# Seven half-size products (Strassen) in place of eight for 42 of the 44 gate/up blocks of a SwiGLU layer

## The chip, the core and the metric

The kernel runs on one core of a Trainium2 chip. The metric is the device time of one execution in microseconds (us), as a median over runs; lower is better. The engines that matter are TensorE (PE, with its weight loads as PEld), VectorE (DVE), ScalarE (ACT), GpSimd (POOL) and the DMA queue that SyncE (SP) feeds. TensorE writes to PSUM, eight banks of 128x512 fp32; all other data lies in SBUF.

## What is computed

One transformer layer on 512 tokens of width 2048 (batch 1, depth 1), fp32 throughout: forgetting attention with four heads, a residual add, then the part that is changed:

```python
D_FF = 5632                                   # -(-8 * 2048 // 768) * 256
h = _rmsnorm(x, norm_ffn)                     # 512 x 2048
gu = h @ w_gate_up                            # 2048 x 11264
g, u = gu[..., :D_FF], gu[..., D_FF:]
x = x + (jax.nn.silu(g) * u) @ w_down         # 5632 x 2048
out = _rmsnorm(x, final_norm)
```

## The kernel before

Every fp32 operand of a matmul is kept as two fp32r parts, high and low: ACT copies it to the high part (a rounding), DVE subtracts the high part from the operand and writes the low part. A product is then three matmuls for each tile of 128 of the contraction: high by high, high by low, low by high (`PASSES`, in `products`, L841). One matmul instruction has a stationary operand of 128x128 and a moving one of up to 512 columns, and each has its own weight load.

The feed-forward part works in 11 groups of 4 blocks. A block is 128 columns of the gate and the same 128 of the up projection. Its result is transposed: 128 features on the partitions, 512 tokens in the columns of a PSUM bank, so that the weights are stationary and the tokens (`hT`, 16 tiles of 128 x 512) move: 2 x 16 x 3 = 96 matmuls of 512 columns. Then ACT takes silu of the gate from its bank into `tmp` (L591), DVE multiplies by the up bank (L817), ACT makes the high part of the activation (L594) and DVE the low part (L820). After four blocks comes the down projection: for each quarter `cb` of the output's 2048 columns and each quarter `tb` of the tokens 4 x 3 matmuls of 512 columns, 192 for a group, and DVE adds each bank to the residual stream `xres` (L772).

Weights come as slabs of 128x2048 fp32 (1 MB): SP loads one into the next of 3 `raw` buffers (L305), ACT (`split_hi`, L422) and DVE (`split_lo`, L617) make the two parts in the next of 2 `split` buffers, and TensorE uses it. A gate slab has all of the contraction, the up slab is the next one, and a down slab is 4 tiles of 128x512. The order on each engine is the order of the code; each engine waits on semaphores that count. The groups run in hardware loops (`Fori`), the first and last apart. In the first group the two slabs of block 0 are multiplied in token halves, matmuls of 256 columns (`EARLY`, `LATE`), because the second half of `hT` (transposed by TensorE at L854, high part L427, low part L624) comes late. After the last group's down projection POOL, ACT and DVE do the final norm: squares (L552), weights (L402), `rstd` (L410), scaling (L803, L807, L584), and 16 stores.

Of the kernel before, what the change touches and what calls it, by code (L numbers as in the profile page):

```python
# [27 lines left out]
P = 128  # L28
SLAB = 2048
# [29 lines left out]

def fox_layer(nc, x, norm_mix, w_in, b_f, w_out, norm_ffn, w_gu, w_down, norm_out, out):  # L60
# [34 lines left out]
    with ExitStack() as ctx:  # L95
# [9 lines left out]

        hT = [sb(f"hT_{n}", [P, ND, S], F32R) for n in ("hi", "lo")]
# [4 lines left out]
        tmp = sb("tmp", [P, 4, BANK])  # L111
        ident = sb("ident", [P, P])
        bound = sb("bound", [P, P])

        with nc.sbuf_tensor("xres", [P, NT, D], F32) as xres, nc.sbuf_tensor("gain", [P, D], F32) as gain:
            pass
# [3 lines left out]
        vT = sb("vT", [P, NH, S])  # L120
        decay_t = sb("decay_t", [P, S], F32R)
        decay_s = sb("decay_s", [P, S], F32R)
        decay_h = sb("decay_h", [P, S], F32R)

        rows = sb("rows", [P, H, 4])
        row_of = sb("row_of", [P, 8])
        head_of = sb("head_of", [P, H])
        wf = sb("wf", [P, ND, H])
        bf_all = sb("bf_all", [P, H])
        bf = sb("bf", [P, 1])  # L130
        half = sb("half", [P, 1])
# [4 lines left out]
        negmax = sb("negmax", [P, NT])  # L136
        rowsum = sb("rowsum", [P, NT])
        rinv = sb("rinv", [P, NT])
# [10 lines left out]

        x_in = [sem(f"x_in{i}") for i in range(NT)]  # L150
# [3 lines left out]
        raw_in = [sem(f"raw_in{i}") for i in range(RAW)]  # L154
        out_done = sem("out_done")
# [46 lines left out]

        y_done = sem("y_done")
# [71 lines left out]

        def wait_used(eng, at):


            n = at.off
            if n < FIRST_WO:  # L280
                eng.wait_ge(slab_used, at.per * at.i + (n + 1))
            elif n < FIRST_FFN:
                cb, second = divmod(n - FIRST_WO, 2)
                if second:
                    eng.wait_ge(y_done, NT * (cb + 1))
                else:
                    eng.wait_ge(slab_used, FIRST_WO + cb + 1)
            else:
                j = n - FIRST_FFN
                if j < 2 * G:  # L290
                    eng.wait_ge(slab_used, (2 * G) * at.i + (FIRST_WO + NC + j + 1))
                else:
                    eng.wait_ge(y_done, (NT * NC) * at.i + (NT * NC + NT * (j - 2 * G + 1)))

        def slab(parts, at, part, tile, cols):

            return parts[part][:, at.ring, tile * cols:(tile + 1) * cols]
# [3 lines left out]
        def _(sp):  # L301
# [32 lines left out]
            with sp.Fori(0, GROUPS) as g:  # L334
                at = At(FIRST_FFN, FFN, g)
                for j in range(2 * G):
                    a = at.plus(j)
                    load(a, tile_of(a, P), w_gu_v[:, :, bass.ds(g * (G * P) + ((j // 2) * P + (j % 2) * F), P)])
                for cb in range(NC):
                    a = at.plus(2 * G + cb)  # L340
                    load(a, tile_of(a, BANK), w_down_v[:, bass.ds(g * G, G), cb * BANK:(cb + 1) * BANK])
# [8 lines left out]
        def _(pool):  # L350
# [47 lines left out]
            for cb, tb in LAST_DOWN:  # L398
                v1 = var[:, tb:tb + 1]
                pool.wait_ge(sq_done, squared(cb, tb))  # L400
                if cb < NC - 1:
                    nc.gpsimd.tensor_tensor(out=y(tb, cb), in0=y(tb, cb), in1=gain[:, cb * BANK:(cb + 1) * BANK],  # L402
# [14 lines left out]
        def _(act):  # L417
# [6 lines left out]
            def take_hT(norm, tb, chunks=range(NC)):  # L424
                for q in chunks:
                    act.wait_ge(h_turned, 4 * NT * norm + 4 * tb + q + 1)
                    nc.scalar.activation(hT[0][:, 4 * q:4 * q + 4, tb * P:(tb + 1) * P],  # L427
# [147 lines left out]
            wait_normalised(act, 1, NT - 1, OWN[1] - 1)  # L575
            wait_normalised(act, 1, NT - 1, NC - 1)
            act.dma_start(gain[:], norm_out.partition_broadcast(P)).then_inc(gain_in, 16)
# [9 lines left out]
            def ffn(g, last=False):  # L587
                at = At(FIRST_FFN, FFN, g)
                for f in range(G):
                    wait_used(act, at.plus(2 * f))  # L590
                    nc.scalar.activation(tmp[:, f % 2, :], ps[:, GU[f % 2][0], :], ACT.Silu).then_inc(silu_done, 1)  # L591
                    split_hi(at.plus(2 * f + 2))
                    act.wait_ge(a_done, G * g + (f + 1))
                    nc.scalar.activation(oT[0][:, f, :], tmp[:, 2 + f % 2, :], ACT.Copy).then_inc(a_hi, 1)  # L594
                    split_hi(at.plus(2 * f + 3))
                if not last:
                    for cb in range(NC):
                        split_hi(at.plus(2 * G + 2 + cb))
                    return
                for cb, tb in LAST_DOWN:  # L600
                    if cb < NC - 2 and tb == 0:
                        split_hi(at.plus(2 * G + 2 + cb))
                    if cb:
                        act.wait_ge(sq_done, squared(cb - 1, tb))
                    square(NT * NC * GROUPS + nth(cb, tb), cb, tb, tmp[:, tb, :])
                    finish_before(cb, tb, finish)

            with act.Fori(0, GROUPS - 1) as g:
                ffn(g)
            ffn(GROUPS - 1, last=True)  # L610
# [3 lines left out]
        def _(dve):  # L614
# [5 lines left out]
            def take_hT(norm, tb):  # L620
                for q in range(4):
                    n = 4 * NT * norm + 4 * tb + q
                    dve.wait_ge(hT_hi, n + 1)
                    nc.vector.tensor_tensor(hT[1][:, 4 * q:4 * q + 4, tb * P:(tb + 1) * P],  # L624
                                            ps[:, turned(norm, tb, q)[0], :].rearrange("p (c t) -> p c t", t=P),
                                            f32(hT[0][:, 4 * q:4 * q + 4, tb * P:(tb + 1) * P]),
# [465 lines left out]
```

## Time and profile before

| what | value |
|---|---|
| median of 3 runs | 1889.2 us (1889.04 to 1890.01) |
| span of the profiled execution, first to last instruction | 1885.3 us |
| matmuls, all with a weight load | 8536 |
| PE busy, PEld busy, DVE busy, ACT busy, POOL busy | 1866.9, 1552.6, 664.1, 474.5, 58.6 us |
| feed-forward part | from about 436 us to the end |
| DMA | 188 MB, 100 GB/s over the span |

The busy time of PE is the union of durations that overlap (one matmul lasts longer than the step to the next), so steps are read from start to start. "Idle before" is the time in which an engine had nothing to run just before an instruction, with the one that released it.

### The profile page before, as it was taken

The page shows a single profiled execution, that of the slowest core. Times are in us where ns is not written, and L with a number is a line of the kernel's source. Part 1 is how long each engine was busy: PE and PEld are TensorE (multiplying, and loading weights), DVE is VectorE, ACT ScalarE, POOL GpSimd, SP SyncE. Part 2 cuts the span into 40 slices and gives each one's busy share as a digit, 9 for nine tenths or more (in the row PEclk, how much of TensorE's full clock was granted, in tenths as well). Part 3 has the DMA queues.
Part 4 walks back from the last instruction along what each step waited for, and adds up shares of the span by engine and source line. Part 5 has one row for each costly group of instructions (what it writes and reads, how often), then busy time and mean ns, then how long its engine had stood idle before and what let it go on. Part 6 is the DMA issues. An engine that isn't in the chain of part 4 may idle for free.

```text
span 1885.3 us, 20299 instructions
## 1 busy us (share of the span) xinstructions
PE 1866.9 (99%) x8536; PEld 1552.6 (82%) x8536; DVE 664.1 (35%) x637; ACT 474.5 (25%) x482; POOL 58.6 (3%) x82
## 2 busy tenths in 40 slices
PE   8999999999999999999999999999999999999998
PEld 6888888888888888888888888888888888888886
DVE  5333332435242242342332332422333333234234
ACT  5223222334212222222222222222221221221224
POOL 3000000012000000000000000000000000000005
PEclk9999999999999999999999999999999999999999
DMA  7333232433333233333233333332333323323322
GB/s 224 90 89 83 73 89 89 179 90 103 99 90 109 92 90 103 97 89 110 90 89 103 97 89 109 92 89 101 99 89 110 90 89 110 90 89 110 91 89 90
DMA packets 266289, 188.22 MB, mean 100 GB/s; under 512 B 5264, under 2 KB 234640, under 8 KB 265360
## 3 DMA queue, kind: packets, MB, share of 16 engines
q1 hardware_dynamic: 263856, 181.45, 32.4%
q10 hardware_dynamic: 2400, 6.29, 0.9%
q8 instruction: 25, 0.41, 0.1%
q14 instruction: 8, 0.07, 0.0%
HBM read 183.54 MB, written 4.19 MB: 100 GB/s over the span
## 4 chain that ended last, share of the span: by engine, by line
PE 96%; DVE 2%; ACT 1%; POOL 1%; issue 1%; DMA 0%; ACTq 0%; POOLq 0%
PE ps L841 95%; DVE tmp L636 1%; POOL xres L402 0%; DVE hT_lo L624 0%; PE ps L854 0%; DMA xres<-in_x_dram 0%; DVE split_lo L617 0%; PE ps L896 0%; DVE xres L772 0%; ACT oT_lo L500 0%; ACT split_hi L422 0%; PE ps L886 0%; ACT hT_hi L427 0%; PE ps L877 0%; ACT tmp L552 0%
## 5 line engine op out<-in xcount | busy, mean ns | idle before, releaser
L841 PE MATMUL ps<-hT_hi,split_hi 128*128 128x512 f32 (+1 forms) x1840 | 706.8, 384 | 0.8 <-DVE split_lo L617 0.8
L841 PE MATMUL ps<-hT_lo,split_hi 128*128 128x512 f32 (+1 forms) x1840 | 706.0, 384 | 0.0
L841 PE MATMUL ps<-hT_hi,split_lo 128*128 128x512 f32 (+1 forms) x1840 | 706.0, 384 | 0.0
L617 DVE TENSOR_TENSOR split_lo<-raw,split_hi 128x2048 fp32r<-128x2048 f32 x164 | 375.9, 2292 | 579.9 <-ACT split_hi L422 579.9
L422 ACT ACTIVATE split_hi<-raw 128x2048 fp32r<-128x2048 f32 x164 | 313.1, 1909 | 378.7 <-PE ps L841 374.8
L841 PEld LDWEIGHTS ps<-hT_hi,split_hi 128*128 128x128 f32 x1840 | 345.9, 188 | 68.4 <-issue 1.0
L841 PEld LDWEIGHTS ps<-hT_hi,split_lo 128*128 128x128 f32 x1840 | 345.9, 188 | 68.0
L841 PEld LDWEIGHTS ps<-hT_lo,split_hi 128*128 128x128 f32 x1840 | 345.9, 188 | 67.6
L841 PE MATMUL ps<-split_hi,oT_hi 128*128 128x512 f32 x832 | 324.3, 390 | 0.6 <-issue 0.4
L841 PE MATMUL ps<-split_hi,oT_lo 128*128 128x512 f32 x832 | 323.9, 389 | 0.0
L841 PE MATMUL ps<-split_lo,oT_hi 128*128 128x512 f32 x832 | 323.9, 389 | 0.0
L772 DVE TENSOR_TENSOR xres<-ps,xres 128x512 f32<-128x512 f32 x192 | 131.0, 688 | 201.1 <-PE ps L841 201.1
L841 PEld LDWEIGHTS ps<-split_hi,oT_hi 128*128 128x128 f32 x832 | 156.2, 188 | 33.6 <-issue 0.8
L841 PEld LDWEIGHTS ps<-split_hi,oT_lo 128*128 128x128 f32 x832 | 156.2, 188 | 32.4
L841 PEld LDWEIGHTS ps<-split_lo,oT_hi 128*128 128x128 f32 x832 | 156.2, 188 | 32.3
L594 ACT ACTIVATE oT_hi<-tmp 128x512 fp32r<-128x512 f32 x44 | 27.8, 632 | 400.1 <-DVE tmp L817 400.1
L817 DVE TENSOR_TENSOR tmp<-ps,tmp 128x512 f32<-128x512 f32 x44 | 30.4, 691 | 265.9 <-PE ps L841 265.9
L591 ACT ACTIVATE tmp<-ps 128x512 f32<-128x512 f32 x44 | 26.3, 598 | 339.1 <-PE ps L841 339.1
L402 POOL TENSOR_TENSOR xres<-xres,gain 128x512 f32<-128x512 f32 x12 | 18.2, 1539 | 1409.2 <-ACT tmp L552 1409.1
L820 DVE TENSOR_TENSOR oT_lo<-tmp,oT_hi 128x512 fp32r<-128x512 f32 x44 | 30.5, 693 | 30.7 <-ACT oT_hi L594 30.7
L678 DVE SCALAR_TENSOR_TENSOR kT_lo<-ps,kT_hi 128x512 fp32r<-128x512 f32 x8 | 5.5, 691 | 60.9 <-ACT kT_hi L466 60.9
L636 DVE SCALAR_TENSOR_TENSOR tmp<-xres,rstd,gain 128x512 f32<-128x512 f32 x20 | 20.9, 1094 | 12.3 <-POOL rstd L387 12.3
(105 smaller groups left out, 454.5 us busy)
## 6 DMA issues: line engine op xcount, KB each, us to landing
raw<-in_ffn_w_gate_up_dram SPq DMA_DIRECT2D x88, 1024.0 KB, 5.7
raw<-in_ffn_w_down_dram SPq DMA_DIRECT2D x44, 1024.0 KB, 5.0
raw<-in_fox_w_in_dram SPq DMA_DIRECT2D x24, 1024.0 KB, 5.8
raw<-in_fox_w_out_dram SPq DMA_DIRECT2D x8, 1024.0 KB, 5.1
xres<-in_x_dram SPq DMA_DIRECT2D x4, 1024.0 KB, 8.2
xres<-in_x_dram ACTq DMA_DIRECT2D x4, 1024.0 KB, 8.5
out_dram<-xres SPq DMA_DIRECT2D x16, 256.0 KB, 3.1
gain<-in_norm_mix_dram SPq DMA_DIRECT2D x1, 1024.0 KB, 6.9
```

Of the source, the lines that this page charges most:

```text
L402: nc.gpsimd.tensor_tensor(out=y(tb, cb), in0=y(tb, cb), in1=gain[:, cb * BANK:(cb + 1) * BANK], op=ALU.mult).then_inc(weighted, 1)
L422: nc.scalar.activation(split[0][:, at.ring, :], raw[:, at.raw, :], ACT.Copy).then_inc(hi_ready, 1)
L591: nc.scalar.activation(tmp[:, f % 2, :], ps[:, GU[f % 2][0], :], ACT.Silu).then_inc(silu_done, 1)
L594: nc.scalar.activation(oT[0][:, f, :], tmp[:, 2 + f % 2, :], ACT.Copy).then_inc(a_hi, 1)
L617: nc.vector.tensor_tensor(split[1][:, at.ring, :], raw[:, at.raw, :], f32(split[0][:, at.ring, :]), ALU.subtract).then_inc(lo_ready, 1)
L636: nc.vector.scalar_tensor_tensor(tmp[:, q, :], y(tb, q), rstd[:, tb:tb + 1], gain[:, q * BANK:(q + 1) * BANK], ALU.mult, ALU.mult).then_in ...
L678: nc.vector.scalar_tensor_tensor(lo, ps[:, PROJ[j % 2], :], SCALE if j < NH else 1.0, f32(hi), ALU.mult, ALU.subtract).then_inc(qk_done, 1)
L772: nc.vector.tensor_tensor(part, ps[:, bank, :], part, ALU.add).then_inc(added, 1)
L817: nc.vector.tensor_tensor(a, ps[:, GU[f % 2][1], :], tmp[:, f % 2, :], ALU.mult).then_inc(a_done, 1)
L820: nc.vector.tensor_tensor(oT[1][:, f, :], a, f32(oT[0][:, f, :]), ALU.subtract).then_inc(a_ready, 1)
L841: ins = nc.tensor.matmul(bank, stationary(sp, t), moving(mp, t), start=first and t == tiles[0] and (sp, mp) == PASSES[0], stop=last and t ...
```

## The change

Block 0 stays as it was (now `early`), and block 1 is multiplied as before, but from slabs of half the size (`plain_part`). The 42 others go through `unit`. Tokens are cut in two halves of 256 and the contraction in two halves of 1024 (A11, A12 for the first tokens, A21, A22 for the others; first digit tokens, second contraction). The weights of a block are cut in the two halves of the contraction and in gate and up (B11, B12 gate and up of the first half, B21, B22 of the second). The seven products (`SEVEN`) are, in order and with the bank that each goes to (numbers relative to a start that rotates by block):

A11·B11 (0), S1·(B11+B12) (1), S2·(B11+B12+B22) (0), S4·B22 (2), S3·(B12+B22) (0), A12·B21 (3), A22·(B11+B12+B22+B21) (0)

with S1 = A21-A22, S2 = S1-A11, S3 = A11-A21, S4 = A12+S2. Bank 0 goes on accumulating over four of them. Each is 8 tiles by 3 passes, 24 matmuls of 256 columns, 168 for a block; the order of the passes is now 16 with the high weights, then 8 with the low ones. The four sums of tokens, with high and low parts, are made once, by DVE and ACT, while blocks 0 and 1 and the first unit run. They lie where the attention's buffers lay (`S1`, `S2` in `oT`, `S3` in `s3`, `S4` in the second ring buffer of `split`); `hT` gets another layout in the second norm (`h_ffn`), and the activations lie over A21.

The sums of weights are four in-place adds of 128x1024 for a block on DVE (`sum_of`, L1231). The high and low parts are made for each of the seven weight operands (`part_hi` L853, `part_lo` L1217, 128x1024) in a ring of two half-size buffers. DVE and ACT combine the products in pieces of 128x256: `copy_q` (L872), four adds or subtractions on DVE (L1282, L1287, L1292, L1297), silu in two halves (L878, L883). SP loads half-size slabs (512 KB) into 6 slots, each load behind a wait on `t_lo` or `t_sum`. The down projection of all groups but the last uses half-size slabs too (two tiles of the contraction for all four `tb`, then the other two); the last one uses full slabs as before. The final gain is now loaded by ACT after the last activation, not at the start of the feed-forward part.

```diff
+        SEVEN = ((A11, 0), (S1, 1), (S2, 0), (S4, 2), (S3, 0), (A12, 3), (A22, 0))
...
+            def half_product(at, e):
+                tokens, which = SEVEN[e]
+                n = at.first + e
+                out = ps[:, bank_of(at.u, which), 0:HALF]
+                fresh = which or e == 0
+                pe.wait_ge(t_hi, at.part(e))
+                for k in range(QK8):
+                    for part in range(2):
+                        ins = nc.tensor.matmul(out, ring(0, n)[:, k * P:(k + 1) * P],
+                                               tokens[part][:, k * HALF:(k + 1) * HALF],
...
+                ins.then_inc(highs_read, 1)
+                pe.wait_ge(t_lo, at.part(e))
+                for k in range(QK8):
+                    ins = nc.tensor.matmul(out, ring(1, n)[:, k * P:(k + 1) * P],
+                                           tokens[0][:, k * HALF:(k + 1) * HALF],
...
+                ins.then_inc(product, 1)
...
+            def part_hi(r, n, source):
+                if n >= 2:
+                    if n - 2 < n_unit_parts(r):
+                        act.wait_ge(highs_read, highs(r, n - 1))
...
+                nc.scalar.activation(ring(0, n), source, ACT.Copy).then_inc(t_hi, 1)
...
+            def unit(at, before, then):
+                if before:
+                    gate_two(before)
+                sum_hi(at, 2)
+                copy_q(at, 0)
+                if before:
+                    act_hi(at.r, before.u, ga[:, :])
+                plain_hi(at.r, at.first + 3, "B22", at.u)
+                copy_q(at, 1)
+                sum_hi(at, 4)
+                plain_hi(at.r, at.first + 5, "B21", at.u)
+                sum_hi(at, 6)
...
+            def part_lo(r, n, source):
+                dve.wait_ge(t_hi, parts(r, n + 1))
+                if n >= 2:
+                    if n - 2 < n_unit_parts(r):
+                        dve.wait_ge(product, products_done(r, n - 1))
...
+                nc.vector.tensor_tensor(ring(1, n), source, f32(ring(0, n)), ALU.subtract).then_inc(t_lo, 1)
...
+            def sum_of(at, into, other):
+                x1, x2 = (slot(place(at.r, name, at.u)[0]) for name in (into, other))
+                nc.vector.tensor_tensor(x1, x1, x2, ALU.add).then_inc(t_sum, 1)
...
-            ffn(0, first=True)
-            with pe.Fori(1, GROUPS - 1) as g:
-                ffn(g)
-            ffn(GROUPS - 1, last=True)
+            for n in range(4):
+                plain_part(n, GU[1][n // 2], n % 2)
+            group(None)
+            with pe.Fori(0, GROUPS - 2) as r:
+                group(r)
```

On TensorE, where one slab or product of a block ends and the next begins. Before, in the last group (`hT` tokens, `split` weights):

```order
L841 MATMUL ps<-hT_hi,split_hi 128x512
L841 MATMUL ps<-hT_lo,split_hi 128x512
L841 MATMUL ps<-hT_hi,split_lo 128x512
L841 MATMUL ps<-hT_hi,split_hi 128x512 [waits lo_ready]
L841 MATMUL ps<-hT_lo,split_hi 128x512
```

The change at the same place, between the first and the second of the seven products (S1 lies in `oT`):

```order
L1635 MATMUL ps<-hT_hi,split_hi 128x256
L1635 MATMUL ps<-hT_lo,split_hi 128x256
L1642 MATMUL ps<-hT_hi,split_lo 128x256 [waits t_lo]
L1642 MATMUL ps<-hT_hi,split_lo 128x256 x7
L1635 MATMUL ps<-oT_hi,split_hi 128x256 [waits t_hi,combined]
L1635 MATMUL ps<-oT_lo,split_hi 128x256
```

The columns of a matmul are halved, and there are two places with waits in each 24 matmuls where there was one in 48.

On DVE, what one block asks for. Before, the block that begins with the second row here, in the last group:

```order
L617 TENSOR_TENSOR split_lo<-raw,split_hi 128x2048 [waits hi_ready]
L817 TENSOR_TENSOR tmp<-ps,tmp 128x512 [waits slab_used,silu_done]
L820 TENSOR_TENSOR oT_lo<-tmp,oT_hi 128x512 [waits a_hi]
L617 TENSOR_TENSOR split_lo<-raw,split_hi 128x2048 [waits hi_ready] x2
```

The change, the first ten operations of a block that follows another (`ga` and `cc` are the gate and up results, `qq` the two copied products):

```order
L1217 TENSOR_TENSOR split_lo<-raw,split_hi 128x1024 [waits product,t_hi]
L1231 TENSOR_TENSOR raw<-raw 128x1024 [waits part_in4,t_lo]
L1254 TENSOR_TENSOR ga<-ga,cc 128x512 [waits silu_done]
L1217 TENSOR_TENSOR split_lo<-raw,split_hi 128x1024 [waits product,t_hi]
L1259 TENSOR_TENSOR hT_lo<-ga,hT_hi 128x512 [waits a_hi]
L1217 TENSOR_TENSOR split_lo<-raw,split_hi 128x1024 [waits product,t_hi]
L1231 TENSOR_TENSOR raw<-raw 128x1024 [waits t_sum]
L1282 TENSOR_TENSOR cc<-qq,ps 128x256 [waits a_done,product,q_copied]
L1217 TENSOR_TENSOR split_lo<-raw,split_hi 128x1024 [waits product,t_hi]
L1287 TENSOR_TENSOR cc<-ps,cc 128x256 [waits combined,product]
```

Two low parts and two operations on the activation became seven low parts, four sums, four combinations and the two operations, each behind a wait on ACT, on TensorE or on DVE itself.

On DVE at the start of the feed-forward part. Before, the last low parts of `hT` are followed by the first low part of weights:

```order
L624 TENSOR_TENSOR hT_lo<-ps,hT_hi 128x4x128 [waits hT_hi] x8
L830 UNCONDITIONAL_BRANCH
L830 ISA
L617 TENSOR_TENSOR split_lo<-raw,split_hi 128x2048 [waits hi_ready]
```

The change, the first of four pieces of the sums of tokens, and the start of the second:

```order
L1015 TENSOR_TENSOR hT_lo<-ps,hT_hi 128x4x128 [waits hT_hi] x8
L1338 TENSOR_TENSOR sy<-hT_hi,hT_lo 128x512 [waits hT_done]
L1338 TENSOR_TENSOR qq<-hT_hi,hT_lo 128x512
L1338 TENSOR_TENSOR sy<-qq,sy 128x512 [waits s_sum]
L1338 TENSOR_TENSOR sz<-hT_hi,hT_lo 128x512
L1343 TENSOR_TENSOR oT_lo<-sy,oT_hi 128x512 [waits s_hi]
L1338 TENSOR_TENSOR sy<-sy,sz 128x512 [waits s_lo,s_sum]
L1338 TENSOR_TENSOR qq<-sz,qq 128x512
L1343 TENSOR_TENSOR oT_lo<-sy,oT_hi 128x512 [waits s_hi]
L1338 TENSOR_TENSOR sy<-hT_hi,hT_lo 128x512 [waits s_lo]
```

Three such pieces stand ahead of the first low part of weights for block 1, and the fourth and S4 between the parts of block 1 and those of the first unit.

## Rows read from the trace of the kernel before

**Rows 1.** The page: busy time by engine, and the chain that ended last

```profile
PE 1866.9 (99%) x8536; PEld 1552.6 (82%) x8536; DVE 664.1 (35%) x637; ACT 474.5 (25%) x482; POOL 58.6 (3%) x82
PE 96%; DVE 2%; ACT 1%; POOL 1%; issue 1%; DMA 0%; ACTq 0%; POOLq 0%
```

**Rows 2.** Busy time in four stretches (start:end length, busy us and count by engine)

```profile
core 0: us, PE busy (x) PEld busy (x) DVE busy (x) ACT busy (x) POOL busy (x), PEclk, DMA share, GB/s
461.80:1832.70 1370.90, 1370.90 (x6050) 1135.53 (x6050) 454.43 (x372) 296.39 (x221) 0.00 (x0) 1.00 0.33 97
```

**Rows 3.** Timeline of PE, block 0 in token halves and its end (start, duration)

```profile
447.60 0.28 PE L841 MATMUL ps<-hT_lo,split_hi 128*128 128x256 f32 x1
447.72 0.28 PE L841 MATMUL ps<-hT_hi,split_lo 128*128 128x256 f32 x1
...
461.75 0.28 PE L841 MATMUL ps<-hT_hi,split_lo 128*128 128x256 f32 x1
461.87 0.40 PE L841 MATMUL ps<-hT_hi,split_hi 128*128 128x512 f32 x1
```

**Rows 4.** Timeline of PE and PEld in an attention head, from 128 to 256 columns

```profile
144.58 0.19 PEld L841 LDWEIGHTS ps<-pT_hi,v_lo 128*128 128x128 f32 x1
144.64 0.27 PE L841 MATMUL ps<-pT_hi,v_lo 128*128 128x128 f32 x1
144.69 0.19 PEld L841 LDWEIGHTS ps<-pT_hi,v_hi 128*128 128x128 f32 x1
144.75 0.33 PE L841 MATMUL ps<-pT_hi,v_hi 128*128 128x256 f32 x1
144.80 0.19 PEld L841 LDWEIGHTS ps<-pT_lo,v_hi 128*128 128x128 f32 x1
144.92 0.28 PE L841 MATMUL ps<-pT_lo,v_hi 128*128 128x256 f32 x1
```

**Rows 5.** Groups by line and shape, DVE (count, busy us, mean ns, idle before)

```profile
L617 DVE TENSOR_TENSOR split_lo<-raw,split_hi 128x2048 fp32r<-128x2048 f32 x164 | 375.9, 2292 | 579.9 <-ACT split_hi L422 579.9
L820 DVE TENSOR_TENSOR oT_lo<-tmp,oT_hi 128x512 fp32r<-128x512 f32 x44 | 30.5, 693 | 30.7 <-ACT oT_hi L594 30.7
L666 DVE TENSOR_TENSOR pT_lo<-ps,pT_hi 128x256 fp32r<-128x256 f32 x4 | 1.7, 415 | 0.0
```

**Rows 6.** The same for ACT

```profile
L422 ACT ACTIVATE split_hi<-raw 128x2048 fp32r<-128x2048 f32 x164 | 313.1, 1909 | 378.7 <-PE ps L841 374.8 <-issue 3.8
L594 ACT ACTIVATE oT_hi<-tmp 128x512 fp32r<-128x512 f32 x44 | 27.8, 632 | 400.1 <-DVE tmp L817 400.1
L456 ACT ACTIVATE pT_hi<-ps 128x256 fp32r<-128x256 f32 x4 | 1.6, 403 | 0.0
```

**Rows 7.** Timeline of ACT and DVE at the start of the feed-forward part

```profile
436.85 1.90 ACT L422 ACTIVATE split_hi<-raw 128x2048 fp32r<-128x2048 f32 x1
438.78 2.29 DVE L617 TENSOR_TENSOR split_lo<-raw,split_hi 128x2048 fp32r<-128x2048 f32 x1 [2.59 <-ACT split_hi L422]
439.88 2.03 ACT L427 ACTIVATE hT_hi<-ps 128x512 fp32r<-128x512 f32 x4
444.40 4.86 DVE L624 TENSOR_TENSOR hT_lo<-ps,hT_hi 128x512 fp32r<-128x512 f32 x8
456.31 0.60 ACT L591 ACTIVATE tmp<-ps 128x512 f32<-128x512 f32 x1 [6.73 <-PE ps L841]
```

**Rows 8.** DMA issues (count, KB each, median us to landing)

```profile
raw<-in_ffn_w_gate_up_dram SPq DMA_DIRECT2D x88, 1024.0 KB, 5.7
raw<-in_ffn_w_down_dram SPq DMA_DIRECT2D x44, 1024.0 KB, 5.0
out_dram<-xres SPq DMA_DIRECT2D x16, 256.0 KB, 3.1
gain<-in_norm_ffn_dram ACTq DMA_DIRECT2D x1, 1024.0 KB, 14.6
```

**Rows 9.** Timeline of PE at the very start, eight equal matmuls twice

```profile
1.30 6.33 PE L934 MATMUL ps<-decay_s 128*128 128x512 f32 x8 [1.30 <-POOL half L352]
12.61 3.60 PE L934 MATMUL ps<-decay_s 128*128 128x512 f32 x8
```

**Rows 10.** The last 8 us, as in rows 2: no matmul, granted clock 0.66

```profile
1878.00:1886.00 8.00, 0.00 (x0) 0.00 (x0) 1.15 (x2) 1.68 (x4) 0.81 (x2) 0.66 0.63 206
```

**Rows 11.** Timeline at the last down projection: DVE, then POOL's first final weight

```profile
1833.04 0.69 DVE L817 TENSOR_TENSOR tmp<-ps,tmp 128x512 f32<-128x512 f32 x1 [6.22 <-PE ps L841]
1846.58 6.48 POOL L402 TENSOR_TENSOR xres<-xres,gain 128x512 f32<-128x512 f32 x4 [1402.65 <-ACT tmp L552]
```

More of the change, by code:

```diff
@@ L333, in _ @@
                 load(a, tile_of(a, BANK), w_out_v[:, kt:kt + NK // 2, cb * BANK:(cb + 1) * BANK])
[L334 to L341, printed above, removed]
+            for j in range(2):
+                load(At(FIRST_FFN + j), tile_of(At(FIRST_FFN + j), P), w_gu_v[:, :, j * F:j * F + P])
@@ new lines, in is_last, with all_units, group @@
+            def is_last(r):
+                return isinstance(r, int) and r == GROUPS - 2
+            def all_units(r):
+                every = units(r)
+                for at, before, then in zip(every, [None] + every[:-1], every[1:] + [None]):
+                    unit(at, before, then)
+            def group(r, following):
+                all_units(r)
+                at = units(r)[-1]
+                gate_two(at)
+                act_hi(r, at.u, ga[:, :])
+                for i in range(2, 2 * NC):
+                    down_hi(r, i)
+                plain_hi(following, 0, "B11", 0)
+                sum_hi(Unit(following, 0), 1)
@@ new lines, in is_last, with all_units, group @@
+            def is_last(r):
+                return isinstance(r, int) and r == GROUPS - 2
+            def all_units(r):
+                every = units(r)
+                for at, before, then in zip(every, [None] + every[:-1], every[1:] + [None]):
+                    unit(at, before, then)
+            def group(r, following):
+                all_units(r)
+                at = units(r)[-1]
+                down_lo(r, 1)
+                act_out(r, at.u, at.silu(2))
+                act_lo(r, at.u, ga[:])
+                for cb in range(NC):
+                    if cb < NC - 1:
+                        down_lo(r, 2 * cb + 2)
+                    else:
+                        unit_lo(Unit(following, 0), 0)
+                        first_sum(Unit(following, 0))
+                    for tb in range(NT):
+                        add(y_before(r) + nth(cb, tb, last=False), cb, SC[tb], tb)
+                    if cb < NC - 1:
+                        down_lo(r, 2 * cb + 3)
@@ new lines, in _, with last_down @@
+            group(None)
+            with pe.Fori(0, GROUPS - 2) as r:
+                group(r)
+            r = GROUPS - 2
+            for at in units(r):
+                unit(at)
+            def last_down(cb, tb, tiles, start=True, stop=True):
+                return products(ps[:, down_bank(cb, tb, True), :],
+                                lambda part, k: aT[part][:, k, tb * P:(tb + 1) * P],
+                                lambda part, k: split[part][:, LAST_RING[cb], k * BANK:(k + 1) * BANK],
+                                tiles, first=start, last=stop)
```

662 lines of the change are left out of this document (556 added, 106 removed), and 3 rows, old and new, of the table LOADS.

## The prediction

> **What bounds the kernel now.** I read the page first: PE is busy 99% of the span and has 96% of the chain that ended last, DVE is busy 35% and ACT 25% [rows 1]. So the time is TensorE's, and busy time says nothing of its pace, since one matmul lasts longer than the step to the next. Hence the stretches: from the end of block 0 to the end of the last block TensorE starts 6050 matmuls in 1370.9 us with no idle time [rows 2]. That is 43 blocks of 96 and 10 down projections of 192, 6048 by the code: a step is 0.2267 us for 512 columns, a block takes 96 x 0.2267 = 21.76 us, a down projection 43.5 us. Then the one place where gate and up are already multiplied with 256 columns, from 447.60 to 461.87: 119 steps in 14.27 us, 0.1199 us each [rows 3]. This is the row on which the gain hangs. Half of 0.2267 would be 0.1133: a matmul has a part of some 0.013 us that doesn't halve.
>
> **The main term.** A changed block has 7 x 24 = 168 matmuls of 256 columns: 168 x 0.1199 = 20.15 us, against 21.76. That is 1.61 us less, not the 2.72 us that an eighth would be. For 42 blocks: 67.8 us. The down projections keep their 192 matmuls of 512 columns; block 0 and block 1 keep theirs.
>
> Can weight loads keep up? A load lasts 0.19 us, more than the new step. But in an attention head loads start every 0.11 us (144.58, 144.69, 144.80) [rows 4], so they overlap, and 0.12 is within their pace, narrowly. Were they unable to, a block would take 168 x 0.188 = 31.6 us; the rows exclude it.
>
> Each product adds two places with waits, 14 for a block, 588 in all. In rows 3 three changes of operand with waits lie inside the 119 steps and are in their mean. The nearest row that speaks for a cost is the step from 144.75 to 144.92, 0.17 us for 256 columns, 0.05 more than the next ones [rows 4]; it comes after 128-column matmuls, where the load was late. I take 0 and keep 0.05 x 588 = 29 us for the range.
>
> The Trainium skill ("TensorE: Matmul & The Clock Gate", Back-to-back issue gap) gives a step of N/2.4 ns plus 2.5 ns. By it 512 columns take 215.8 ns and 256 take 109.2 ns, and 42 blocks would save 42 x (20.72 - 18.35) = 99.6 us. The trace doesn't agree: 226.7 and 119.9 ns.
>
> **Can DVE and ACT feed it?** Durations: DVE 2.292 us for 2048 columns, 0.693 for 512, 0.415 for 256 [rows 5]; the line through the first two gives 1.23 for 1024. ACT 1.909, 0.632 and 0.403 [rows 6], so 1.06 for 1024. Bounds for 1024 on DVE: half of 2.292 (1.15) and two of 512 (1.39). Per block DVE does 7 low parts, 4 sums, 4 combinations, and the product and low part of the activation: 11 x 1.23 + 4 x 0.42 + 2 x 0.69 = 16.6 us of 20.15 (82%). ACT: 7 x 1.06 + 4 x 0.40 + 0.63 = 9.7 us. Both fit, so what decides is the order. I lay out one block, TensorE's product e beginning at 2.88e. Its high weights are free at +1.92, its bank is readable at +3.05 (a matmul's end is 0.16 after the next step); the high part of e+2 waits for the first, the low part of e+2 for the second.
> - From the block before: product 5 readable at -2.7, combination to -2.3, low part of product 0 to -1.05, first sum to 0.2.
> - ACT high part 1 to 1.3, DVE low 1 to 2.5, second sum to 3.7.
> - ACT high part 2 to 4.8 (needed at 5.76), the copy of product 0 to 5.2 (needed at 5.76: slack 0.6), DVE multiplies the old activation meanwhile, low 2 to 6.0 (needed 7.7).
> - ACT high 3 to 6.8, DVE low 3 to 8.0 (needed 10.6), third sum to 9.2, ACT high 4 to 10.3 (needed 11.5), low 4 to 11.5.
> - Product 3 is readable at 11.7, and from here DVE waits for TensorE again: low 5 to 13.3 (needed 16.3), fourth sum 14.6, ACT high 6 to 15.6 (needed 17.3).
>
> TensorE waits for nothing; the smallest slack is 0.6 us and is built on eleven hand-overs. A hand-over is short: ACT ends at 438.75 and DVE begins at 438.78, and DVE kept its 2.29 us while ACT worked beside it [rows 7]. DMA: the loads for the next block are issued at 9.2 to 14.6 and needed 13 us later; a half slab must land between the 3.1 us of 256 KB and the 5.7 us of 1 MB [rows 8]. In the down projection a half slab is worth 5.4 us of TensorE, against one high part, one low part and two adds for it; hidden. I take 0 for the steady state.
>
> **The start.** DVE is free at 449.3 (444.40 + 4.86) [rows 7]; TensorE needs the first parts of block 1 at 461.87 [rows 3]. Ahead of them stand three of four pieces of token sums. A piece is 9 operations of 0.69 and, since nearly each waits for ACT or for the one before, about 6.4 us: 449.3 + 5.6 + 6.4 + 6.4 = 467.7; then ACT's copies of the last S3 piece and of the first weights: 469.3. TensorE waits 7.4 us. After it blocks run to 491.1. DVE goes on: two low parts (471.9), the fourth piece and S3 (479.4), activation of block 0, and two low parts with four pieces of S4 of about 3.5 us (three operations, a copy, a low part), first weights of the unit, a sum, activation of block 1: 500.3. ACT has the second high part at 499.9, so the unit's second product begins there and not at 494.0, and the third at 504.1 after sum, high part and copy. Without waits the third would begin at 461.87 + 21.76 + 5.76 = 489.4. Loss: 14.7 us. DVE's whole list here is some 45 us of work; at the 0.60 of eight low parts in 4.86 us [rows 7] it is 5 us shorter, and with 0.1 more for each of 52 hand-overs 5 us longer: 9 to 20 us.
>
> The clock: after some 4 us without a matmul it had fallen at the end (0.66 over 8 us in which the last matmul had ended about 1876.5, the rest at full speed) [rows 10], which is from 2.4 to 1.2 GHz. At the start eight equal matmuls took 6.33 us, later 3.60 [rows 9]: a restart costs 2.7 us. After the first wait that falls into the second one and costs nothing; after the second, 3.5 us long by then, 0 to 2.7. I take 0.
>
> **The end.** DVE has in its list the low part of the second full down slab (2.29 us) ahead of the low part of the last activation: 1.6 us after the last product ACT has silu, then 1.9 of high part, 0.6 of activation, and DVE is done about 5.7 us after the last product, where TensorE has two banks of nine matmuls, 4.1 us, to go on with. Loss 1.5 us; before there was none. The final gain is issued about 3.5 us after the last product and needed by POOL 13.8 us after (1846.58 against 1832.8) [rows 11]: 6.9 us would do, 14.6 [rows 8] would be 4 late, on a POOL list that lies near the end. I take 0, keep 4.
>
> **Sum.** -67.8 + 14.7 + 1.5 = -51.6 us. On the profiled span, 1885.3 to 1833.7; the median lies 3.9 us over the span, so 1837.6, say 1838 us.
>
> **Rivals.**
> - *The waits between products show.* Each costs about 0.05 us, or the 0.6 us of slack in a block is used up by hand-overs and TensorE waits 0.5 to 0.7 us in each block: +21 to +29, 1859 to 1867 us. For it: two operations at each point where there was one in 48 matmuls, register arithmetic in the loop, three engines in turn. Against: 0.1199 includes waits.
> - *The step halves.* With the tokens now contiguous and the weights high ones first, 0.1133 us: 168 x 42 x 0.0066 = 46 us less, 1792. Rows 3 speak against it, since the same instruction takes 0.1199 there. The 109.2 ns of the Trainium skill's page would go this way too.
> - *DVE becomes the bound, and it is slower than before.* Mechanism: from product 5 of a block to high part 4 of the next DVE has seven operations of 1024 in a row, with three high parts on ACT between them, and 1.2 us of slack (10.3 against 11.5). Above 1.40 us for an operation on DVE TensorE waits in each block; at 1.58 us it waits 1.23 us, and 42 of these take all of the 51.6. At 1.65 us: 7 x 0.42 - 1.2 = 1.74, x 42 = 73, so 1911 us. It would take an add in place, or DVE under ACT, PE and DMA at once, to be a third slower than the line of rows 5. Against: rows 7, and the upper bound of 1.39 us, at which nothing waits yet.
>
> **How the numbers follow.** Forecast 57%, its own range 1828 to 1852 (start 9 to 20, clock 2.7, gain 4, step 0.1195 to 0.1203). Waits that show 22%. Step halves 6%. DVE bound and slower than before 9%. The other 6% is a mix between forecast and before. 0.2% (3.8 us) is about what can be told from no change. Faster 0.89, same 0.02, slower 0.09. The range leaves out the halved step, the slower case and the far end of the waits: 1823 to 1872.
>
> **What would show it.** 11,560 matmuls (8536 + 42 x 72), a step of 0.120 in the units, 20.15 us from block to block in a group and 124.1 us for a group (130.6 now); DVE busy about 1150 us, from 664. PE idle in two gaps near 462 and 494, 7.4 and 3.5 to 6 us, with the clock down after the first. A wait of TensorE on DVE or ACT that recurs in each block would be the third rival; steps of 0.12 with a longer one at each first matmul the first. If TensorE's idle time is small and the span is still above 1850, the step is wrong.

## The result, and the profile after

The median goes from 1889.1 us to 1840.3 us (four runs of each, 1838.7 to 1841.4 after); the ratio is 0.974, 95% interval 0.973 to 0.976. The forecast was 1838, its range 1823 to 1872. The profiled execution has a span of 1839.3 us.

First the page of the changed kernel, as in [rows 1]: busy time by engine, and by engine the chain (the work that ended last, followed back from the end of the span):

```profile
PE 1807.1 (98%) x11560; PEld 1647.4 (90%) x11560; DVE 1115.5 (61%) x1277; ACT 659.0 (36%) x867; POOL 58.5 (3%) x82
PE 92%; DVE 4%; ACT 2%; issue 1%; POOL 1%; DMA 0%; ACTq 0%; POOLq 0%; DVEq 0%
```

The 11,560 matmuls are there, and the chain has still 92% on TensorE. Where it waits is in the view of waits (engine, line, waited for: us in total, times, longest):

```profile
PE ps L1617 <- ACT split_hi L853: 7.5, 1, 7.5
PE ps L1635 <- ACT split_hi L853: 4.8, 1, 4.8
...
PE ps L1423 <- DVE hT_lo L1259: 1.0, 1, 1.0
```

These three are new; each happens once, none recurs by block. Five stretches of the span (start:end length, PE busy and matmuls, granted clock, share of DMA, GB/s): up to block 0's last steps, those, on to the first down projection, on to the last one, and the rest. The cuts at 542.60 and 1785.43 come from the chain, where a piece begins as the matmul before it ends; the first matmul of these two down projections starts at 542.43 and 1785.32:

```profile
0.00:461.60 461.60, 451.71 (x2278) 0.99 0.37 107
461.60:463.83 2.23, 2.23 (x20) 1.00 0.00 0
463.83:542.60 78.77, 66.40 (x435) 0.91 0.27 81
542.60:1785.43 1242.83, 1242.78 (x8641) 1.00 0.35 102
1785.43:1839.30 53.87, 43.96 (x193) 0.96 0.36 126
```

From 542.60 on TensorE is never idle for 1243 us. The third row holds the loss: one plain block and two changed ones would be 21.76 + 2 x 20.16 = 62.1 us, and from 463.83, where block 0 is through, to 542.43 it took 78.6, so 16.5 us are lost there. Beside the kernel before: up to the end of block 0 the profiled run is 1.96 us longer (463.83 against 461.87 [rows 3]), from there to the last down projection 1321.5 us against 1370.9 [rows 2], and the rest 1.45 us longer. The sum is the -46.0 us of the spans. Most of the first is not the change's: 36 matmuls of the attention part took 6.08 us here (granted clock 0.79 from 20 to 28 us) and 4.58 before (1.00). Five of the ten kernels below that are built from the changed one had 4.58 or 4.59 again, and the first two below, built from the kernel before, had 6.07 and 6.09.

The chain of the changed kernel inside one group shows the pace (start, us, what); a product is 16 matmuls on the high weights and 8 on the low ones:

```profile
603.42 1.92 PE ps L1635 x16
605.34 0.96 PE ps L1642 x8
606.30 1.92 PE ps L1635 x16
608.22 0.96 PE ps L1642 x8
...
626.45 1.92 PE ps L1635 x16
```

A product is 2.88 us, a block of seven (606.30 to 626.45 in the chain) 20.15 us, a step 0.120 us, and no hand-over shows. 192 matmuls of a down projection remain at 43.55 us.

### The profile page after: what moved, and what is told of

It reads as the page before. It is cut to its first block, busy times and chain, and to the rows that moved or that the text cites. A ratio compares the mean times of both kernels' runs of the same rounds, so it can differ in the third digit from the quotient of the medians.

```text
span 1839.3 us, 29804 instructions
## 1 busy us (share of the span) xinstructions
PE 1807.1 (98%) x11560; PEld 1647.4 (90%) x11560; DVE 1115.5 (61%) x1277; ACT 659.0 (36%) x867; POOL 58.5 (3%) x82
## 4 chain that ended last, share of the span: by engine, by line
PE 92%; DVE 4%; ACT 2%; issue 1%; POOL 1%; DMA 0%; ACTq 0%; POOLq 0%; DVEq 0%
PE ps L1423 45%; PE ps L1635 31%; PE ps L1642 15%; DVE tmp L1027 1%; DVE hT_lo L1015 1%; DVE qq L1338 1%; POOL xres L656 0%; DVE sy L1338 0%; PE ps L1436 0%; DVE oT_lo L1343 0%; ACT split_hi L853 0%; DMA xres<-in_x_dram 0%; DVE split_lo L1217 0%; DVE split_lo L1008 0%; PE ps L1478 0%
## 5 line engine op out<-in xcount | busy, mean ns | idle before, releaser
L853 ACT ACTIVATE split_hi<-raw 128x1024 fp32r<-128x1024 f32 x378 | 399.9, 1058 | 781.8 <-DVE raw L1231 387.7
L1217 DVE TENSOR_TENSOR split_lo<-raw,split_hi 128x1024 fp32r<-128x1024 f32 x378 | 462.0, 1223 | 331.5 <-ACT split_hi L853 331.5
L1423 PE MATMUL ps<-split_hi,hT_hi 128*128 128x512 f32 x704 | 274.2, 389 | 1.0 <-DVE hT_lo L1259 1.0
L1423 PE MATMUL ps<-split_lo,hT_hi 128*128 128x512 f32 x704 | 274.0, 389 | 0.0
L1423 PE MATMUL ps<-split_hi,hT_lo 128*128 128x512 f32 x704 | 273.9, 389 | 0.0
L1635 PE MATMUL ps<-hT_hi,split_hi 128*128 128x256 f32 x1008 | 247.8, 284 | 0.0
L1231 DVE TENSOR_TENSOR raw<-raw 128x1024 f32<-128x1024 f32 x168 | 205.2, 1221 | 9.6
L1423 PE MATMUL ps<-hT_hi,split_hi 128*128 128x512 f32 (+1 forms) x464 | 171.2, 369 | 0.8 <-DVE split_lo L1008 0.8
L1423 PE MATMUL ps<-hT_hi,split_lo 128*128 128x512 f32 (+1 forms) x464 | 170.4, 367 | 0.0
L1423 PE MATMUL ps<-hT_lo,split_hi 128*128 128x512 f32 (+1 forms) x464 | 170.4, 367 | 0.0
L1008 DVE TENSOR_TENSOR split_lo<-raw,split_hi 128x2048 fp32r<-128x2048 f32 x34 | 77.9, 2291 | 119.6 <-ACT split_hi L676 119.6
```

The costliest lines, as they stand in the source:

```text
L853: nc.scalar.activation(ring(0, n), source, ACT.Copy).then_inc(t_hi, 1)
L1008: nc.vector.tensor_tensor(split[1][:, at.ring, :], raw[:, at.raw, :], f32(split[0][:, at.ring, :]), ALU.subtract).then_inc(lo_ready, 1)
L1217: nc.vector.tensor_tensor(ring(1, n), source, f32(ring(0, n)), ALU.subtract).then_inc(t_lo, 1)
L1231: nc.vector.tensor_tensor(x1, x1, x2, ALU.add).then_inc(t_sum, 1)
L1423: ins = nc.tensor.matmul(bank, stationary(sp, t), moving(mp, t), start=first and t == tiles[0] and (sp, mp) == PASSES[0], stop=last and t ...
L1635: ins = nc.tensor.matmul(out, ring(0, n)[:, k * P:(k + 1) * P], tokens[part][:, k * HALF:(k + 1) * HALF], start=bool(fresh) and k == 0 and ...
```

## Experiments

The median of the kernel before, measured again beside the experiments, was 1887.8, 1889.1 and 1888.5 us. So a difference of about 1 us between two kernels measured at different times shows nothing by itself.

**What halving the columns costs.** The kernel before, gate/up slabs in two halves, then in four quarters.

```diff
-  project(at.plus(2 * f + up), GU[f % 2][up]).then_inc(slab_used, 1)
+  project(at.plus(2 * f + up), GU[f % 2][up], EARLY)
+  project(at.plus(2 * f + up), GU[f % 2][up], LATE).then_inc(slab_used, 1)
```

> The kernel before, with every gate/up slab multiplied in two token halves of 256 columns: eight half-size products, no Strassen, so no weight sums and no token sums; 192 matmuls of 256 columns per block in place of 96 of 512. Theory (a matmul has a part that does not halve, step 0.1199 us at 256 columns): a block takes 192 x 0.1199 = 23.02 us, 1.26 more than 21.76, over 43 blocks about +54 us, so about 1943 us; seven eighths of that block is the 20.15 us forecast for the changed one. Rival (the step halves, 0.1133 us, and what is missing from an eighth was lost to something else in the changed kernel): 192 x 0.1133 = 21.76, no change, 1889 us.

Measured: 1966.0 us against 1887.8, ratio 1.041 (1.039 to 1.043). The chain of this kernel, one turn of its loop over groups:

```profile
712.36 1.06 issue
713.42 1.69 PE ps L841 x12
715.11 1.34 issue
716.46 134.52 PE ps L841 x948
850.98 1.06 issue
```

134.52 us hold 756 half-size matmuls and a down projection: (134.52 - 43.55) / 756 = 0.1203 us for one. A block then takes 23.10 us, and 43 blocks +58 us. That is the theory; the rival (no change) is out. The other 19.3 us of the +78 are in rows that nobody expected: at each of the eight places where the loop turns back TensorE is idle twice for "issue", for 0.9 to 1.2 us and, 12 matmuls later, for 1.1 to 1.6 us. The changed kernel has 864 matmuls in its loop where this one has 960, and no such gap. Seven eighths of 23.10 are 20.2 us, as measured.

The quarters use `slice(quarter * P, (quarter + 1) * P)` in the same place, four times.

> The kernel before with every gate/up slab multiplied in four quarters of 128 columns: 384 matmuls per block. It asks how far matmuls can be made smaller, as a second level of half-size products would need. Theory A (weight loads start every 0.11 us at the least, as in the attention head of the kernel before): 384 x 0.11 = 42.2 us for a block, +20.5, over 43 blocks about +880 us, so about 2770 us. Theory B (only the line through 0.2267 us at 512 and 0.1199 at 256 columns, which gives 0.0665 at 128): 25.5 us for a block, +3.8, so about 2052 us. Under A the 0.1199 us of 256 columns lies only 8% above the floor of the loads.

Measured: 3432 us in a single run, more than either said. Two stretches, each of one group (length, PE busy and matmuls, granted clock):

```profile
852.20:1067.50 215.30, 215.26 (x1728) 1.00 0.20 60
1068.60:1440.00 371.40, 371.40 (x1728) 0.56 0.12 35
```

The first confirms theory A: (215.3 - 43.55) / 1536 = 0.112 us for 128 columns, as close as weight loads follow each other [rows 4]. The second has the same work at a lower clock: after 1.0 us of idle time at the loop's turn the granted clock is 0.63 over 12 us, then 0.50 (1.2 GHz) for the rest of the quarter-size products, though TensorE is never idle; it is 1.00 again some 5 us into the down projection. Four groups went this way, 156 us each, and why these four is open. With 43 blocks of 42.94 us in place of 21.76 (911 us), four times 156 (624 us) and 8 us of idle time the +1544 us are accounted for. So a second level of halving would gain nothing: 0.112 is hardly less than 0.120.

**The start.** Does the loss belong to the token sums?

```diff
-  [flat(oT[part])[:, 0:SLAB] for part in range(2)], [flat(oT[part])[:, SLAB:2 * SLAB] for part in range(2)],
-  [s3[part][:, :] for part in range(2)], [split[part][:, 1, :] for part in range(2)])
+  [quarter(part, 0, 0) for part in range(2)], [quarter(part, 0, 1) for part in range(2)],
+  [quarter(part, 1, 1) for part in range(2)], [quarter(part, 0, 0) for part in range(2)])
...
-  for i in range(3):
-      sum_piece(i)
...
-  fourth_piece(0)
```

> The changed kernel without the sums of token halves: they are not computed, and the products that should read them read plain token halves in their place (same sizes, same counts; so the output is another one). Everything else, the weight sums included, stays. Theory (the 16.5 us lost near the first changed block is DVE's and ACT's list of token sums and the conversions queued behind it): both waits go, -15 to -17 us, about 1824 us. Rival 1 (the loss is the order of first weights and a cold start in this place, whatever the sums cost): at most half goes, -8 us or less. Rival 2: the table load of ACT and the conversions alone keep the second wait: -7.5 us for the first wait and nothing for the second, about 1833.

TensorE's waits for the sums went with them, and ACT got three waits for low parts in their place. Measured: 1825.6 us, 14.7 less than with them and just short of the 15 to 17; the span is 1823.4, 15.9 less. Its chain has no wait at this place:

```profile
449.54 14.40 PE ps L1410 x120
463.94 3.65 PE ps L1604 x16
...
526.04 34.03 PE ps L1410 x150
```

Block 0 to the first down projection is 62.1 us, where the changed kernel has 78.6. The 16.5 us are the sums' and their queue's; both rivals are out.

Is it the order in that list, or its length? The first weights one piece earlier, on ACT and DVE alike:

```diff
-  for i in range(3):
+  for i in range(2):
       sum_piece(i)
   named_lo(None, 0, "gate", 0)
   named_lo(None, 1, "gate", 1)
+  sum_piece(2)
```

> The changed kernel with one change of order on DVE and ACT: the first two weight parts of block 1 are converted behind the second piece of the token sums in place of behind the third. Theory (the length of DVE's list to the first unit sets the loss, not its order): TensorE begins block 1 at about 465 in place of 471.5 and waits the time again in its middle or after it; the third product of the first unit still starts at about 508, so 0 (-1 to +1), about 1840. Rival (the first wait is a loss of its own): -5 to -6.5.

Measured: 1841.2 us, 0.9 more than the changed kernel, inside the scatter. Its waits on TensorE:

```profile
PE ps L1619 <- ACT split_hi L853: 8.6, 2, 7.5
PE ps L1637 <- ACT split_hi L853: 4.2, 1, 4.2
```

The first wait fell from 7.5 to 1.1 us, and 7.5 came back in the middle of block 1, whose second half of weights still stood behind the sums. An order moves the wait about; only less to do, or more time for it, takes it away.

How much of it is the clock? 38 multiplications that nobody reads are to keep TensorE busy in its second wait:

```diff
   pe.wait_ge(s_lo, 12)
+  for k in range(38):
+      nc.tensor.matmul(ps[:, bank_of(at.u, 1), 0:HALF], A12[0][:, 0:P], A12[0][:, 0:HALF],
+                       start=True, stop=True, skip_group_check=True)
```

> The changed kernel with 38 multiplications of 256 columns that nobody reads, put on TensorE ahead of the second product of the first unit, where it waits 4.8 us. Theory (1.6 us of the start's loss is the lowered clock after this wait: that product takes 4.45 us in place of 2.88): the clock stays up, the product takes 2.88 us and the time falls by 1.6 us. Rival (third product waits for its high part, converted on ACT at 506.1 to 507.1, whatever the second one takes): about 0.

Measured: 1839.5 us, 0.8 less, not to be told from nothing by the times alone. In the changed kernel the stretch from 503.40, behind the wait, had a granted clock of 0.51; in this kernel it is 1.00:

```profile
503.40:506.20 2.80, 2.77 (x13) 0.51 0.00 0
```

```profile
503.40:506.20 2.80, 1.81 (x16) 1.00 0.00 0
```

The product is fast now, but the next one waits 1.0 us for ACT's copy of product 0, which ACT makes right behind the high part that the rival named. It begins at 506.21 in place of 507.88, and 1.26 of these 1.67 us are an earlier DVE (its multiplication of the activation at 501.72, not 502.98; in this profiled run all of the feed-forward part lies 1.3 us earlier, from the attention part on). So the clock was worth 0.4 us, and the rival holds for the rest of the 1.6.

**The slack in a block.** One more DVE instruction ahead of each of the four weight sums, with 256, 512 or 1024 columns; its result is used by nobody.

```diff
   x1, x2 = (slot(place(at.r, name, at.u)[0]) for name in (into, other))
+  j = (("B11", "B12"), ("B11", "B22"), ("B12", "B22"), ("B11", "B21")).index((into, other))
+  nc.vector.reduce_max(var[:, j:j + 1], x2[:, 0:256], AX)
   nc.vector.tensor_tensor(x1, x1, x2, ALU.add).then_inc(t_sum, 1)
```

> The changed kernel with one more DVE instruction ahead of each of the four weight sums of a unit (a maximum over 256 columns of the sum's second operand; its result is used by nobody): some 0.33 us each (d), 1.3 us per unit, so DVE goes from 61% to 64% busy. Theory (order decides: two sums and two extra operations lie ahead of the copy of product 0, which has 0.4 us of slack; three extra ahead of high part 4, with 1.0): TensorE waits the larger of 2d-0.4 and 3d-1.0, 0.26 us, in each of 41 units, about +9 to +11 us. Rival (sum of work decides, 20.15 us a unit with some 13 used): nothing shows, 0.

> As extra_256, with 512 columns, about d = 0.6 us each, 2.4 us per unit (DVE about 67% busy by sum). Theory (order decides): the larger of 2 x 0.6 - 0.4 and 3 x 0.6 - 1.0 is 0.8 us a unit, +34 us, about 1874. Rival (sum of work decides): 13.3 + 2.4 is 15.7 of 20.15 us, nothing shows, 1840.

> As extra_256, with 1024 columns, about d = 1.13 us each, 4.5 us per unit (DVE 73% busy by sum). Theory (order decides): 3 x 1.13 - 1.0 = 2.4 us a unit, +98 us, about 1940, slower than the kernel before. Rival (sum of work decides): 13.3 + 4.5 is 17.8 of 20.15 us, nothing or a few us show.

Measured: 1862.1, 1892.6 (ratio to before 1.002, 1.001 to 1.003) and 1984.2 us, so +21.8, +52.4 and +143.9 where the theory said 10, 34 and 98. The rival is out: with four times 0.60 us of DVE work more in a block of 20.15 the whole gain is gone. The theory was short by one sum. Per block the loss is 0.52, 1.25 and 3.4 us; all four added operations less about 1.0 us come near that (4 x 0.34, 4 x 0.60 and 4 x 1.13 give 0.4, 1.4 and 3.5), three of them less 1.0 don't (0, 0.8 and 2.4). The smallest loss also fits the two operations ahead of the copy of product 0: in the changed kernel ACT has this copy done at 611.68 and TensorE begins product 2 at 611.89, so 2 x 0.34 less 0.2 is 0.5. This fit was made after the fact. The waits of the kernel with 512 columns name the place, the copy of product 0, once a block:

```profile
PE ps L1637 <- ACT qq L872: 41.1, 40, 1.5
```

Why all four count is in the changed kernel's own timeline, DVE in one block (start, duration, idle time before and releaser):

```profile
603.46 0.43 DVE L1297 TENSOR_TENSOR ga<-ps,qq 128x256 f32<-128x256 f32 x1 [0.55 <-PE ps L1642]
603.80 1.22 DVE L1217 TENSOR_TENSOR split_lo<-raw,split_hi 128x1024 fp32r<-128x1024 f32 x1
605.14 1.23 DVE L1231 TENSOR_TENSOR raw<-raw 128x1024 f32<-128x1024 f32 x1
607.66 1.23 DVE L1217 TENSOR_TENSOR split_lo<-raw,split_hi 128x1024 fp32r<-128x1024 f32 x1 [1.29 <-ACT split_hi L853]
...
616.83 1.23 DVE L1217 TENSOR_TENSOR split_lo<-raw,split_hi 128x1024 fp32r<-128x1024 f32 x1 [0.87 <-ACT split_hi L853]
...
621.86 1.23 DVE L1217 TENSOR_TENSOR split_lo<-raw,split_hi 128x1024 fp32r<-128x1024 f32 x1 [0.71 <-ACT split_hi L853]
623.61 0.42 DVE L1297 TENSOR_TENSOR ga<-ps,qq 128x256 f32<-128x256 f32 x1 [0.53 <-PE ps L1642]
```

Of the 4.1 us that DVE is idle in a block, 3.6 end at ACT and 0.5 at TensorE. The reading is this: sum, ACT's high part, low part and next sum are one chain through two engines, so the 3.6 us are part of the chain and no slack in it. By the losses above this chain takes some 19.2 us (20.15 less 1.0) of each block. Two experiments test this reading. In the first 512 columns stand behind the sum, where DVE mostly waits for ACT anyway (they are columns of the tokens, not of the slab; the instruction lasts 0.68 us in both places):

```diff
   nc.vector.tensor_tensor(x1, x1, x2, ALU.add).then_inc(t_sum, 1)
+  nc.vector.reduce_max(var[:, j:j + 1], f32(A11[0])[:, 0:512], AX)
```

> The changed kernel with the same four extra DVE instructions per unit as in extra_512 (maximum over 512 columns, result used by nobody), but each right behind its weight sum in place of ahead of it: there DVE waits 0.7 to 1.3 us for ACT's high part in any case. Theory (the slack belongs to the chain of hand-overs DVE sum, ACT high part, DVE low part, and not to DVE's sum of work): the 0.6 us lie in those waits, 0 to +4 us, about 1842. Rival (it is DVE's sum of work, or its port, that extra_512 filled): +52 as there, about 1892.

In the second DVE has nothing to do in addition, but ACT has, between a sum and its high part (`extra` is a tile of its own, not read):

```diff
   act.wait_ge(t_sum, at.sums((0, 1, 2, 0, 3, 0, 4)[e]))
+  nc.scalar.activation(extra[:], f32(A11[0])[:, 0:256], ACT.Copy)
```

> The changed kernel with one extra ACT instruction (a copy of 256 columns, used by nobody; about 0.35 us) in front of each of the four high parts that wait for a weight sum, behind that wait; DVE has nothing more to do and ACT is 36% busy. Theory (the chain through both engines has about 1.0 us of slack a unit): 4 x 0.35 - 1.0 = 0.4 us a unit, +16 to +22, about 1860, as much as the same length on DVE costs. Rival (DVE's own list is the limit, ACT has 12 us free in a unit): 0.

Measured: 1841.3 us (+1.0, no difference) and 1856.1 us (+15.9, by the theory +16 to +22; the rival, 0, is out). The same 1000 us, 700 to 1700, of three kernels (PE, PEld, DVE, ACT busy and counts): the changed one with 512 columns ahead of the sums, the one with them behind, and the one with more on ACT:

```profile
700.00:1700.00 1000.00, 966.25 (x6717) 903.98 (x6717) 712.94 (x839) 342.81 (x436) 0.00 (x0) 1.00 0.33 97
```

```profile
700.00:1700.00 1000.00, 1000.00 (x6938) 937.63 (x6937) 738.92 (x865) 360.49 (x450) 0.00 (x0) 1.00 0.35 102
```

```profile
700.00:1700.00 1000.00, 994.92 (x6888) 929.97 (x6887) 662.18 (x736) 395.65 (x575) 0.00 (x0) 1.00 0.35 101
```

DVE is busy 74% where TensorE never waits, and 71% where it waits 3% of the time; ACT at 40% holds TensorE up. Busy shares say nothing here, the chain through both engines does.

**Better versions.** The end alone, the last activation's parts ahead of the second full down slab's:

```diff
-  last_lo(1)
   act_lo(at.r, at.u, ga[:])
+  last_lo(1)
```

> The changed kernel with DVE's and ACT's lists changed at one place: ahead of the last down projection the high and low parts of the last activation come before those of the second full down slab, so that TensorE's 1.0 us wait for the low part of the hidden tile goes. Theory: the wait goes and nothing else is late, because the second full slab is needed only 96 matmuls (21.8 us) later: -1.0 us. Rival: the final gain or the slab is late in turn and the 1.0 us comes back there: 0.

Measured: 1839.8 us, 0.45 less, which the times alone don't show. The traces are clearer. The last down projection in the changed kernel, then in this one:

```profile
1787.69 2.29 DVE split_lo L1334
1789.99 0.61 DVE hT_lo L1259
1790.60 0.04 issue
1790.64 17.99 PE ps L1423 x78
```

```profile
1785.45 21.93 PE ps L1423 x96
1807.39 0.02 issue
```

96 matmuls end at 1807.4 and not at 1808.6: the wait is gone, with 0.2 us of slow steps behind it, and nothing else is late.

The start, with three plain blocks, with first weights ahead of token sums, and the end as above:

```diff
-  for i in range(3):
-      sum_piece(i)
-  named_lo(None, 0, "gate", 0)
-  named_lo(None, 1, "gate", 1)
-  sum_piece(3)
...
+  sum_piece(0)
+  named_lo(None, 1, "gate", 0)
+  named_lo(None, 2, "gate", 1)
+  sum_piece(1)
...
+  named_lo(None, 3, "up", 0)
+  sum_piece(2)
+  named_lo(None, 4, "up", 1)
+  sum_piece(3)
```

> The changed kernel with three plain blocks ahead of the first changed one in place of two (41 changed ones), the first weights of block 1 converted ahead of the token sums, and the order at the end as in the kernel 'end'. Theory: block 1 starts without a wait and the token sums and their queue lie beside one more plain block; one changed block less costs 1.6 us, so -16.5 + 1.6 - 1.0 = about -16, about 1824 us. Rival: the list of DVE (some 45 us) still ends after the third plain block does, because the first weights of three blocks and two activations are in it as well, and 3 to 6 us of the wait stay: -10 to -13.

Measured: 1828.1 us, 12.2 less than the changed kernel; ratio to before 0.968 (0.967 to 0.969). It beats both kernels. The forecast of -16 missed, the rival's -10 to -13 held. Its waits from block 0 on:

```profile
PE ps L1651 <- DVE split_lo L1237: 0.7, 1, 0.7
PE ps L1664 <- ACT qq L878: 0.7, 1, 0.7
PE ps L1646 <- ACT split_hi L859: 0.5, 1, 0.5
PE ps L1664 <- ACT split_hi L859: 0.4, 1, 0.4
```

Block 1 begins at 461.97 and the first down projection at 529.28: 67.3 us for two plain blocks and one changed one, which are 63.7. So 3.6 us of 16.5 stay, 2.3 in these waits and the rest in slower first steps after them. The 12.9 us saved less 1.6 for the block, 11.3, and about 1 at the end are the 12.2. Three edits came together here; the order at the start and the order at the end were also run alone, the third plain block was not.

## Why the prediction was right

- **The pace.** Forecast 0.1199 us a step, 20.15 us a block, 124.1 us a group. Measured 0.120, 20.15, 124.2. The line through [rows 3] held, and the half-size kernel without Strassen gives the same 0.120. The halved step is out (0.1133 us), and with it the 99.6 us by the Trainium skill's "TensorE: Matmul & The Clock Gate" (Back-to-back issue gap): the page gives its formula as the gap of a single matmul, and the 109.2 ns that it makes for 256 columns no trace here shows.
- **Waits between products.** Taken as 0, kept to 29. Measured: none between the products of a group, only 0 to 0.25 us more in the first 16 matmuls behind a down projection; with that and blocks of 20.16 in place of 20.15 the steady part is some 1.8 us over its sum. The 0.17 of [rows 4] was a late load, not a wait's price.
- **DVE and ACT feed it.** DVE 1115.5 us, forecast 1150; an operation of 1024 took 1.22 us, by the line 1.23. The slack at the copy of product 0 was to be 0.6; ACT has it done at 611.68, 5.55 after the product began (606.13), so 0.2. The slack for all of a block was to be 1.2 and is about 1.0 by the extra operations. The third rival is thus real, and 2.4 us of DVE work a block away: the kernel with 512 columns is where it sets in as slower than before. What the sum had wrong is where slack lies: it laid out seven operations from product 5 to high part 4, but the fourth sum is in the same chain.
- **The start.** Forecast 14.7 us, measured 16.5, to the third product (507.88 in place of 491.35) as to the down projection; the two waits 7.4 and 3.5 to 6, measured 7.5 and 4.8. Two terms make up nearly all of the 1.8 us: the clock behind the second wait, taken as 0, was 0.4, and the sum had no term for a table that ACT loads for its first silu. The chain that ended last runs through this load, ahead of the weights that DVE waits for; no run took it away. ACT's timeline of the changed kernel:

```profile
480.85 1.28 ACT L969 ACT_TABLE_LOAD   x1
482.14 0.60 ACT L969 ACTIVATE ga<-ps 128x512 f32<-128x512 f32 x1
```

In the kernel before the same load stood in time in which ACT waited for TensorE, and cost nothing:

```profile
448.29 1.28 ACT L591 ACT_TABLE_LOAD   x1
```

The Trainium skill ("ScalarE activation tables: per-element evaluation and per-set limits", What a function is on this engine) gives 1283 ns for it; the trace agrees, with 1.28 us.

The clock behind the first wait cost block 1 2.3 us (24.04 from 471.53 to 495.57) and was covered by the second wait, as forecast.
- **The end.** Forecast 1.5, measured 1.2 by the kernel without it. The final gain was not late: POOL's first use of it, at 1800.50, waited for ACT's squares, as before.
- **The sum.** -67.8 + 16.5 + 1.8 + 1.2 is -48.3 us; the medians differ by 48.8, the spans of the profiled runs by 46.0 with 2.0 us of cold matmuls in the attention part. The forecast was -51.6: the start was 1.8 us more and the steady part 1.8, the end 0.3 less. So each term was right to 2 us, and only 0.3 us of the misses cancel. The profiled span, forecast at 1833.7, is 1839.3 because the 2.0 us of the attention part come on top of these 3.3.

## What to carry to other kernels

An eighth fewer products at half the size gave 7% per block, not 12.5%, because the 0.013 us of a matmul that did not halve (by the line through 512 and 256 columns) came twice as often: read the step at the new size from a place in the trace where it already occurs, before counting operations saved. Where two engines hand work to each other, add up the chain through both, and don't count as slack the idle time in which one of them waits for the other. A one-time preparation on an engine that had been idle lies on the path if the first use follows soon; one more plain block to hide behind, with the first weights ahead of it, cost 1.6 us and saved 12.9; the order alone had saved nothing.

## What the runs showed that was not expected

- A loop body of 960 matmuls left TensorE idle twice at its start on every turn, 0.9 to 1.2 and 1.1 to 1.6 us, one of 1728 matmuls once a turn, 0.8 to 1.0 us; with 864 there was nothing. Each matmul has a weight load of its own, so these are 1920, 3456 and 1728 instructions. By the Trainium skill ("Runtime: NRT & Kernel Launch", Instruction fetch mechanics) TensorE's instruction store holds 2048 instructions, they are fetched ahead in sequence only, and a taken branch to a target outside of the current window of two pages (256 instructions each) stalls for a fetch. The three loops fall on either side of a limit somewhere from 1728 to 1920. That would agree with a store of 2048 if waits and branches fill the rest, and not with a window of 512, which the loop without a gap exceeds as well. That a fetch is the cause no run here shows.
- In a stream of 128-column matmuls, each step 0.112 us, the granted clock fell to 0.50 after four of the loop's eight idle turns (0.97 to 1.03 us; the other four, 0.84 to 1.01, had no such effect) and stayed there for the rest of a group's products (371 us in place of 215), though TensorE was busy throughout. The same idle time between 256-column matmuls had no such effect.
